# Gathering two expert tables as one: u and v rows side by side in a DRAM table, and weights made two slots at a time

## The reference, cut to what matters

```python
def block(xc):                       # 128 tokens at a time
    q = (xc @ w_q).reshape(T, 8, 2, 128)
    s = einsum('thsd,hsnd->thsn', q, sub_keys)       # 2 x 128 key scores a head
    s1, i1 = top_k(s[:, :, 0], 16); s2, i2 = top_k(s[:, :, 1], 16)
    cand = s1[..., None] + s2[..., None, :]          # 16 x 16 pairs
    top_s, pos = top_k(cand, 16)                     # idx: 16 of 16384 experts a token and head
    gate = softmax(top_s)
    act = gelu(einsum('thkd,td->thk', u_emb[idx], xc))
    return einsum('thk,thkd->td', gate * act, v_emb[idx])
```

## Time and profile before

| | |
|---|---|
| median of 3 runs | 2135.82 us (2129.47 to 2137.36) |
| the profiled execution, its own time | 2135.21 us |
| its span, first to last instruction | 2133.1 us |
| mean granted TensorE clock, share of full | 0.944 |
| PE, PEld, DVE, ACT, POOL busy | 1786.3, 974.6, 1432.5, 534.8, 1168.6 us |
| moved by DMA | 603.05 MB: 537.99 on POOL's queue, 63.85 on SP's |

### The profile page before, as it was taken

How to read it: one execution, slowest core, us unless ns; L and a number is a source line. 1 busy time by engine, 2 the same in 40 slices (tenths; PEclk the granted TensorE clock), 3 DMA queues, 4 the chain that set the end, 5 groups by cost and what they waited for, 6 DMA issues and landing times.

```text
span 2133.1 us, 19325 instructions
## 1 busy us (share of the span) xinstructions
PE 1786.3 (84%) x5959; PEld 974.6 (46%) x5959; DVE 1432.5 (67%) x2983; ACT 534.8 (25%) x1207; POOL 1168.6 (55%) x1171
## 2 busy tenths in 40 slices
PE   5988799999999969978788789878868977887687
PEld 5546434778997754423333233323323323332233
DVE  5598774444443488777777786687677777777763
ACT  3334443222333231212211221121112111311211
POOL 6990000000000077777777777777777777777773
PEclk9998899999999989999999889989989999999899
...
GB/s 121 57 23 20 109 1 35 99 95 151 85 135 109 1 335 385 379 402 396 407 409 409 406 409 408 406 409 405 403 404 405 399 409 409 409 409 404 401 404 249
DMA packets 239390, 603.05 MB, mean 283 GB/s; under 512 B 38533, under 2 KB 105274, under 8 KB 239290
## 3 DMA queue, kind: packets, MB, share of 16 engines
q0 software_dynamic: 147840, 537.99, 64.0%
q1 hardware_dynamic: 91450, 63.85, 10.8%
...
## 4 chain that ended last, share of the span: by engine, by line
PE 39%; POOL 20%; DVE 15%; DMA 13%; issue 9%; ACT 3%; SPq 1%; DVEq 0%; ACTq 0%; POOLq 0%
PE bank L1562 19%; PE bank L1875 16%; POOL R L2002 13%; DMA R<-in_peer_v,R 4%; POOL WS L2002 3%; DMA WS<-in_peer_u,R 3%; DVE R L990 3%; PE bank L1853 3%; POOL slabs L2002 3%; DMA slabs<-in_peer_u,R 2%; DMA R<-in_peer_u,R 2%; DVE R L1449 1%; PE bank L1551 1%; DVE stat L1248 1%; DVE R L1403 1%
## 5 line engine op out<-in xcount | busy, mean ns | idle before, releaser
L1875 PE MATMUL bank<-R 128*128 128x512 f32 x2048 | 976.6, 627 | 231.6 <-ACT R L928 153.2
L1875 PEld LDWEIGHTS bank<-R 128*128 128x128 f32 x2048 | 391.9, 199 | 805.3 <-issue 600.1
L2002 POOL DMA_INDIRECT R<-in_peer_v,R x512 | 509.6, 995 | 162.2 <-issue 138.4
L2002 POOL DMA_INDIRECT WS<-in_peer_u,R x172 | 174.0, 1011 | 640.7 <-DVEq L1437 588.5
L1449 DVE CUSTOM_DVE_ANT_0 R<-WS,XN 128x1024 f32<-128x1024 f32 x172 | 210.7, 1225 | 98.7 <-DMA WS<-in_peer_u,R 93.5
L1449 DVE CUSTOM_DVE_ANT_0 R<-slabs,XN 128x1024 f32<-128x1024 f32 x168 | 205.8, 1225 | 98.6 <-DMA slabs<-in_peer_u,R 93.7
L1449 DVE CUSTOM_DVE_ANT_0 R<-R,XN 128x1024 f32<-128x1024 f32 x172 | 210.7, 1225 | 88.3 <-DMA R<-in_peer_u,R 82.8
L1562 PE MATMUL bank<-R 128*64 128x64 f32 (+6 forms) x792 | 193.7, 393 | 33.7 <-ACT R L708 11.6
L2002 POOL DMA_INDIRECT R<-in_peer_u,R x172 | 180.1, 1047 | 52.4 <-issue 52.4
L921 ACT ACTIVATE R<-R 128x16 f32<-128x16 f32 x32 | 6.9, 216 | 780.0 <-DVE R L1449 780.0
L2002 POOL DMA_INDIRECT slabs<-in_peer_u,R x168 | 169.9, 1011 | 56.5 <-issue 50.6
...
## 6 DMA issues: line engine op xcount, KB each, us to landing
...
slabs<-in_w_mem_kv SPq DMA_DIRECT2D x8, 1024.0 KB, 5.6
slabs<-in_w_peer_q SPq DMA_DIRECT2D x8, 1024.0 KB, 16.5
R<-in_peer_v,R POOLq DMA_INDIRECT x512, 12.3
slabs<-in_w_in SPq DMA_DIRECT2D x4, 1024.0 KB, 14.4
...
slabs<-in_w_out SPq DMA_DIRECT2D x4, 1024.0 KB, 5.1
slabs<-in_w_mem_q SPq DMA_DIRECT2D x4, 1024.0 KB, 5.2
```

The lines of the kernel that those rows point to most:

```text
L1875: last = pe.matmul(ps[2 * (t % 2) + n][:, :], diag[s % DRING], Vb[i % VRING][:, 512 * n:512 * n + 512], start=(s == 0), stop=(s == TOPK - 1))
L2002: pool.indirect_dma_start(out=dst, out_offset=None, in_=table, in_offset=bass.IndirectOffsetOnAxis(ap=ix[:, s:s + 1], axis=0)).then_inc(si ...
```

## The change

1. A DRAM table `UV` of 16384 rows x 8 KB is made in the kernel. After `output_matrices(3)` POOL issues 32 transfers from DRAM to DRAM, each 1024 rows of 4 KB (4 MB): u into the left half of the rows, v into the right. They are 134.2 MB read and 134.2 MB written. Before its first gather POOL waits for all of them (`uv_in`).
2. One indirect DMA a slot fetches 128 rows of 8 KB, 512 of them in place of 1024. The two rings of 12 buffers of 4 KB a partition become one ring of 12 buffers of 8 KB; a buffer is free when PE has summed its v half.
3. Weights are made for two slots at a time: `weigh(g, b)` on ACT waits for two dots, makes two gelus, two products with the gate and two diagonals. DVE's `weights` goes. The dots of a group are now made in the same group as its sums, around the two halves of the top-k (`sub_keys`, `pairs`), and PE takes a slot as soon as its diagonal is there; the query products are spread one between slots.
4. The order of the last memory-output products, their banks and some buffers change, group 0's slots go in between them, and `final_root` of all four tiles comes last.

```diff
--- before.py
+++ after.py
...
 SLAB = 2048
-URING, VRING = 12, 12
+RING = 12
 DRING = 16
+COPY_ROWS = 1024
 
 
...
@@ -159,7 +160,7 @@
     j += [("mo", 1, 0), ("p0", 0, 0), ("p0", 0, 1), ("mo", 1, 1), ("q0", 0), ("s0", 0)]
     j += [("mo", 1, 2), ("mo", 1, 3), ("mo", 2, 0), ("mo", 3, 0)]
     j += [("p0", 1, 0), ("p0", 1, 1), ("mo", 2, 1), ("q0", 1), ("s0", 1)]
-    j += [("mo", 3, 1)] + [("mo", t, n) for n in (2, 3) for t in (2, 3)]
+    j += [("mo", 3, 1), ("mo", 2, 3), ("mo", 3, 3), ("mo", 2, 2), ("mo", 3, 2)]
     j += [("pT", k) for k in range(KD)]
     return j
 
...
-        OmT = [OmT01[:, 0], OmT01[:, 1], reg(8704, KD, P), reg(19456, KD, P)]
+        held = sb("held", P, D)
+        OmT = [OmT01[:, 0], OmT01[:, 1], held[:, :].rearrange("p (k n) -> p k n", k=KD), reg(19456, KD, P)]
...
@@ -514,11 +519,14 @@
 
 
         qw = slab(("pq", 0), 8, 256)
-        Ub = [WS[:, D * i:D * i + D] for i in range(4)] + [reg(15360 + D * i, D) for i in range(4)]
+        UV = nc.dram_tensor("uv_rows", [NK * NK, 2 * D], F32, kind="Internal").ap()
+        rings = [WS[:, 2 * D * i:2 * D * i + 2 * D] for i in range(2)] + \
+            [reg(at, 2 * D) for at in (7168, 9216, 11264, 13312, 15360, 17408)]
         for n in range(2):
             at = SLAB * (slab_no[("mo", n)] % SLOTS)
-            Ub += [slabs[:, at + D * i:at + D * i + D] for i in range(2)]
-        assert len(Ub) == URING
+            rings.append(slabs[:, at:at + 2 * D])
+        rings += [reg(at, 2 * D) for at in (3072, 5120)]
+        assert len(rings) == RING
 
         block = ctx.enter_context(nc.Block())
 
@@ -916,34 +924,32 @@
                 act.wait_ge(gates_neg, g + 1)
                 act.activation(ex, cv, ACT.Exp, bias=nmx, accum_out=esum).then_inc(gates_exp, 1)
 
-            def gelu_of(g):
-                act.wait_ge(dots, (g + 1) * TOPK)
-                act.activation(gel, act_row, ACT.Gelu_apprx_tanh).then_inc(gelu_done, 1)
-
-            def diagonals(g, t, first=False, slots=range(TOPK)):
-                act.wait_ge(w_ready, g + 1)
-                for s in slots:
-                    if not first:
+            def weigh(g, b):
+
+                if b == 0:
+                    act.wait_ge(gate_ready, g + 1)
+                act.wait_ge(dots, g * TOPK + (2 * b + 2))
+                two = slice(2 * b, 2 * b + 2)
+                settle(act.activation(gel[:, two], act_row[:, two], ACT.Gelu_apprx_tanh))
+                for s in (2 * b, 2 * b + 1):
+                    ins = act.activation(wgt[:, s:s + 1], gel[:, s:s + 1], ACT.Copy, scale=gate[g % NT][:, s:s + 1])
+                settle(ins)
+                for s in (2 * b, 2 * b + 1):
+                    if g:
                         act.wait_ge(v_summed, g * TOPK + (s - DRING + 1))
-                    act.activation(diag[s % DRING], ident, ACT.Copy,
-                                   scale=wgt[t % 2][:, s:s + 1]).then_inc(diag_done, 1)
+                    act.activation(diag[s], ident, ACT.Copy, scale=wgt[:, s:s + 1]).then_inc(diag_done, 1)
 
             def head(h, first=False, last=False):
                 for t in range(1 if first else 0, NT):
                     g = h * NT + t
-                    if t < 2 and not last:
-                        queries_out(h + 1, t)
-                    if not last or t < 2:
-                        gate_exponentials(g + 2)
-                    if last and t == NT - 1:
-
-                        diagonals(g, t)
-                        final_root(0)
-                        final_root(1)
-                    else:
-                        diagonals(g, t)
-                    if not last or t < NT - 1:
-                        gelu_of(g + 1)
+                    for b in range(TOPK // 2):
+                        if first and (t, b) == (1, 2):
+                            queries_out(1, 0)
+                        if b == 6 and t < 2 and not last and not (first and t == 0):
+                            queries_out(h + 1, t)
+                        if b == 7 and (not last or t < 2):
+                            gate_exponentials(g + 2)
+                        weigh(g, b)
 
             def final_root(t):
                 act.wait_ge(var_done, len(PARTS) + t + 1)
...
             for h in range(1, PH - 1):
                 head(h)
             head(PH - 1, last=True)
-            final_root(2)
-            final_root(3)
+            for t in range(NT):
+                final_root(t)
 
 
         @block.vector
@@ -1414,10 +1423,13 @@
                                           ps[6 + s][:, P * t0:].rearrange("p (t n) -> p t n", n=NK)))
                 dve.sem_inc(s_copied, 1)
 
-            def topk(t):
+            def sub_keys(t):
 
                 for s in range(2):
...
@@ -1436,24 +1448,20 @@
                 lstep(dve.scalar_tensor_tensor(idx[t], isel[:, 0:16], float(NK), isel[:, 16:32], ALU.mult, ALU.add))
                 dve.sem_inc(idx_ready, 1)
 
-            def gates_of(g, t):
+            def gates_of(g):
                 dve.wait_ge(gates_exp, g + 1)
                 lstep(dve.reciprocal(rinv, esum))
-                lstep(dve.tensor_scalar(gate[t % 2], ex, rinv, None, ALU.mult))
-
-            def dot_products(g, t, slots=range(TOPK)):
+                lstep(dve.tensor_scalar(gate[g % NT], ex, rinv, None, ALU.mult))
+                dve.sem_inc(gate_ready, 1)
+
+            def dot_products(g, t, slots):
 
                 for s in slots:
                     i = g * TOPK + s
-                    dve.wait_ge(ld_u[i % URING], (i // URING + 1) * 16)
-                    dve.tensor_tensor_reduce(prod, Ub[i % URING], xn[:, t, :], 1.0, 0.0, ALU.mult, ALU.add,
+                    dve.wait_ge(ld_uv[i % RING], (i // RING + 1) * 16)
+                    dve.tensor_tensor_reduce(prod, rings[i % RING][:, 0:D], xn[:, t, :], 1.0, 0.0, ALU.mult, ALU.add,
                                              act_row[:, s:s + 1]).then_inc(dots, 1)
                     dve.wait_ge(dots, g * TOPK + (s + 1))
-
-            def weights(g, t):
-                dve.wait_ge(gelu_done, g + 1)
-                lstep(dve.tensor_tensor(wgt[t % 2], gel, gate[t % 2], ALU.mult))
-                dve.sem_inc(w_ready, 1)
 
             def take_sum(g, t):
 
@@ -1468,16 +1476,19 @@
                 for t in range(1 if first else 0, NT):
                     g = h * NT + t
                     ahead = not last or t < 2
+                    dot_products(g, t, range(0, 5))
                     if t == 2 and not last:
                         scores(h + 1)
                     if ahead:
-                        topk((t + 2) % NT)
+                        sub_keys((t + 2) % NT)
+                    dot_products(g, t, range(5, 8))
                     take_sum(g + (-1), (t - 1) % NT)
-                    if not last or t < NT - 1:
-                        dot_products(g + 1, (t + 1) % NT)
-                        weights(g + 1, (t + 1) % NT)
+                    dot_products(g, t, range(8, 10))
                     if ahead:
-                        gates_of(g + 2, t)
+                        pairs((t + 2) % NT)
+                    dot_products(g, t, range(10, TOPK))
+                    if ahead:
+                        gates_of(g + 2)
 
             def final_variance(t):
 
...
@@ -1823,6 +1838,17 @@
             mem_out(1, 0)
             early_turns(0)
             mem_out(1, 1)
+            def slots(g, t, some):
+
+                for s in some:
+                    i = g * TOPK + s
+                    pe.wait_ge(diag_done, g * TOPK + (s + 1))
+                    v = rings[i % RING]
+                    for n in range(2):
+                        last = pe.matmul(ps[2 * (t % 2) + n][:, :], diag[s], v[:, D + 512 * n:D + 512 * n + 512],
+                                         start=(s == 0), stop=(s == TOPK - 1))
+                    last.then_inc(v_summed, 1)
+
             for q in range(4):
                 await_drained(pe, ("keyT", q))
             await_slab(pe, ("pq", 0))
@@ -1835,24 +1861,28 @@
             mem_out(2, 1)
             early_query(1)
             mem_out(3, 1)
-            for n in (2, 3):
-                for t in (2, 3):
-                    mem_out(t, n)
+            mem_out(2, 3)
+            mem_out(3, 3)
+            slots(0, 0, range(0, 2))
+            mem_out(2, 2)
+            mem_out(3, 2)
+            slots(0, 0, range(2, 6))
             pe.wait_ge(xn_done, before[4])
             for k in range(KD):
                 turn(("pT", k), lambda b: [(b[:, columns(t)], xn[:, t, columns(k)]) for t in (2, 3)])
             for k in range(KD):
                 await_drained(pe, ("pT", k))
 
-            def queries(h, s, first=False):
-
-                if s == 0 and not first:
+            def queries(h, s, first=False, ks=range(KD)):
+
+                if s == 0 and ks[0] == 0 and not first:
                     pe.wait_ge(qw_in, h * 16)
                 cols = slice(2 * P if first else 0, T)
-                for k in range(KD):
```

(113 more changed lines are left out.)

89 lines of the change are left out of this document (48 added, 41 removed).

## The result

| | before | after |
|---|---|---|
| median (lowest to highest of 4 runs) | 2136.59 us (2129.47 to 2139.65) | 2298.06 us (2290.42 to 2302.47) |
| ratio, 95% interval | | 1.0764 (1.0743 to 1.0785): slower |
| span of the profiled execution | 2133.1 us | 2298.5 us |
| first gather | 748.08 us | 945.14 us (+197) |
| first gather to the end | 1385.0 us | 1353.4 us (-32) |

+197 - 32 = +165 us is the whole difference of the spans (165.4). The forecast had the same two terms as +400 and -10. The direction came as forecast and the time lies in the range (2190 to 2620), but 161 us were lost where 390 were forecast, and the time is outside the likeliest case's own bounds (2440 to 2600): it is that of rival R3. Where some runs of a kernel were slower at a lower clock, the ratios in this document are made without them.

A forecast was written before the change was run, and what follows sets the result against it. The prediction took the encoder as bound by PE and what feeds it, the retrieval by transfers at 409 GB/s. From 2135 us, +400 for encoder loads delayed by copies and -10 for the gathers gave 2525 us, range 2190 to 2620.

The forecast's parts named there:

- likeliest case: Encoder loads and copies take turns one for one, a copied row at 0.28 to 0.32 us: 2440 to 2600 us, chance 0.48.
- R3: Copies beside loads: one-for-one turns, but a cheap copied row of 0.16 to 0.22 us; 2245 to 2355 us, chance 0.17.
- a copied row holds an engine for 0.320 us: DRAM-to-DRAM copies: 2048 rows for each DMA engine, 0.320 us each as upper end, 656 us in all; lower end 0.160.
- R2: Loads get through, gathers wait for the copies: first gather 68 to 225 us late, 2193 to 2350 us, chance 0.15.
- The turns: SP's loads while copies are queued: each run of a load waits one copy row more, 0.320 us (lower end 0.160).
- R4: Engines take turns by whole runs of rows, so the encoder stands until the copies end: about 2750 us, chance 0.07.
- DTm: Encoder loads of DTm, 64 runs an engine for each q: +17 us for q = 3, +11 for q = 2, together +28.
- w_uq and positions: Encoder loads on the chain before the attention, 584 runs an engine at 0.320 us: +187 us (lower end +93).
- Attention as cover: The attention, about 125 us, hides the next loads, x and the first two slabs, 92 us: +0.
- The mix loop: Encoder iterations, 224 runs an engine each, take 77 us for 19.6 until copies end near 870 us; total delay then +400.
- The gathers: Retrieval: no gain from 8 KB rows at 409 GB/s; shorter end -34, slower start +24, taken as -10 us.
- R1: Copies hidden in the encoder, rows at most 0.21 us, runs losing well under 0.05: 2125 down to 2101 us, chance 0.13.

The follow-up runs named there:

- experiment 4: Kernel after, gathers taken from u as 8 KB rows, with the 32 copies issued alone after the last sum: 2560.62 us, one run.
- Experiment 1: Kernel after without the 32 copies and their wait, 8 KB rows gathered out of u itself: 2107.61 us, 0.9856 of before.
- paced kernel: Kernel after with the copies in 64 transfers of 512 rows, issued a few after each encoder stage, none during w_uq and positions: 2151.14 us, 0.9386 of before.

## Why the prediction came out as it did

**The step that failed** is the term "a copied row holds an engine for 0.320 us". The prediction bounded it by 0.160 and 0.320 and took the upper end, since a read and a write both pass DRAM. It measures 0.185 to 0.204 us (after, experiment 4), near the lower end. The doubling was an argument without a row: the earlier trace rows give a row's price as the time for which it holds a DMA engine, and nothing in the trace of before says that the write adds a second such time. Measured, it adds at most 0.044 us; that the write overlaps the read fits this, but no run shows it. The page of the Trainium skill that was cited (DMA: Bandwidth & Descriptors, Latency and other measured facts) has 207 to 214 GB/s for copies between HBM tensors, of another shape and on other queues; here the copies move 319 and 297 GB/s beside loads (3.19 MB in 10 us, 8.91 in 30) and 294 to 316 alone, and for them the measurement decides. That the time still lies in the range is luck as far as the likeliest case goes: it is held by the part of the range that was there for R2 and R3.

**The turns were right.** "One copy row more for each run of a load" holds to the packet: 790 and 790, 2208 and 2208. With 0.203 in it the prediction's own step gives 584 x 0.203 = 119 us for w_uq and the positions, against 116 measured. R4, whole runs of rows, is out: its 64 rows against 8 runs would not give equal counts. The 9 to 17 descriptors that an engine drains before it changes queues (the Trainium skill, DMA: Bandwidth & Descriptors, Queues, rings and completion order) were not seen between these two queues either: the first transfer of DTm, 8 runs an engine, would have been through in one turn, and took eight (1.43 us against 0.52 without copies). The earlier trace rows already had the rule, and the new slab time repeats it: (25.2 - 5.6) / 64 = 0.306 us a run, one 8 KB row (2.49 us / 8 = 0.311).

**DTm** +31 against +28. This is near by luck. q = 3 lost 17 us as forecast (from 213.27 to 247.00 us where it was 199.11 to 216.13; 1.4 of it in PE's product, 10.52 for 9.16 us) and q = 2 lost 14 against 11, though a row took two thirds of the time charged. For q = 3 the 64 runs at 0.203 are 13 us of the 23 from Y(2)'s end to the landing, where the forecast's 25 had 20 for them; SP's eight issues (5 us) and a slow start of the turns (160 runs in all from 214 to 220 us) make up for it. **w_uq and positions** +116 against +187, the row alone. **Attention as cover**: right, 378.84 to 502.7 us is 124 us against 125. **The mix loop** +50 against +185 (400 - 187 - 28): a turn of 0.217 makes an iteration 224 x 0.217 = 49 us and not 77, so an iteration that meets copies throughout loses 29 us where 57 were charged (measured: 27 for the third, 12 for the second, which still had a slab in store), and the copies end at about 640 us, not 870, so that the next two lose only 3 and 5. The cheap row counts twice there, which is why 37% off in the row (0.320 to 0.203) is 51% off in the delay.

**The gathers** -32 against -10. The prediction said that no row showed a faster slice, and took nothing; the 8 KB rows move at 421 GB/s, above the 410 that it named as a sign that this term is wrong. 512 x 1.049 MB is 1275 us at 421 and 1313 at 409: 38 us less. At the start the ring of 12 costs about what was foreseen, 22 us against 24 (385 GB/s from 945 to 1200 us, 359 of it from 1000 to 1100). Experiment 1 has the same term without the copies: 2107.61 against 2137.76.

**R1** was nearer than its 0.13 said on one of its two conditions, the row (0.20 where it decides at 0.21), and wrong on the other: each run lost 0.2 us, not "well under 0.05". **R2** is out: the gathers are released by the indices. **R3** is what happened, 2245 to 2355 us for 0.16 to 0.22 us; it had a chance of 0.17. With both bounds a factor of two apart and no row at either, a middle value for the unknown row would have been the better choice: R3's own steps gave 2355 for 0.22.

What stays open: where the 46 us of the paced kernel go in detail, and why the kernel before is slower on two of the three chips (on C in its 4 KB gathers; of B there is no profile of it).
